# Two blocks of transformer layers on one core: half of some low weight parts on GpSimd, MLP sums kept in PSUM, all modulation sums on VectorE

## The chip, the cores and the metric

The kernel runs on one core of one Trainium2 chip. The metric is device time in microseconds (us) of one execution; lower is better. A difference of over 0.3% is about what a measurement of this kernel can tell.

## What is computed

Two blocks, one after the other, on a sequence of 256 tokens of width 1024, in float32.

The first block has two layers. Each is an adaptive norm (RMS norm, then a scale and a shift that come from a condition vector), an input projection of 4352 columns, two kinds of attention with 8 heads each, gates, an output projection, a second adaptive norm and an MLP of width 4096 with a squared ReLU. Cut to what matters here:

```python
mod = silu(c) @ w_ada + b_ada                  # 1024 x 6144: six chunks of 1024
sh1, sc1, gt1, sh2, sc2, gt2 = split(mod, 6)
h = rms_norm(x, g_mix) * (1 + sc1) + sh1
proj = h @ w_in                                # q, k, v of two attentions, two gates
mixed = sigmoid(gate_a) * (att_a @ w_o_swa) + sigmoid(gate_b) * (att_b @ w_o_moba)
x = x + gt1 * (mixed @ w_out)
h = rms_norm(x, g_mlp) * (1 + sc2) + sh2
x = x + gt2 * (square(relu(h @ w_up)) @ w_down)
```

The second block (a pooling layer and an attention layer, each with a mixture of experts) reads the result and a context of 256 more tokens. Its modulations are `silu(c) @ w_mod` for the tokens and `silu(c_ctx) @ w_mod` for the context. They depend on the inputs alone, so the kernel computes most of them while the first block runs.

## The kernel before, in words

**Units.** All weights come from HBM as 1 MB units, each 1024 rows by 256 columns (128 partitions x 2048 elements). Units 0 to 56 are layer 0 and 57 to 113 layer 1 of the first block: 9 of query, key and value projections, 8 of gates (with the attention beside them), 4 of the two attention outputs (each unit makes `y_a` and `y_b` of 256 columns), 4 of `w_out` ("out units") and 32 of the MLP. Unit 114 begins the second block.

**Two parts of a product.** A float32 product is made of three products of a rounded type: high x high, high x low and low x high. For each weight unit ScalarE writes the high part of the raw weights (L1449, `w_hi`, 128x2048), then VectorE subtracts it from the raw ones and writes the low part in two halves (L1946, `w_lo`, 128x1024 each). TensorE needs 48 matmuls of 256 columns for a unit (function `product`, L773). Three units can be split at a time (`w_hi`, `w_lo` have three places). Activations are split in the same way: ScalarE writes `h_hi`, `u_hi`, VectorE `h_lo`, `u_lo`.

**Modulations.** Each condition vector times a modulation matrix is done in pieces of 256 rows by 1024 columns (1 MB, an item `mod, layer, chunk, pair`; four pairs make a chunk; modulation layers 0 and 1 are `w_ada`, 2 and 3 are `w_mod`). For an item VectorE multiplies the two 128-row halves by the condition's columns and adds them into an accumulator (first one L1963, a `tensor_scalar`; the others L1969, a `scalar_tensor_tensor` from `raw` and `acc` into `acc`, 128x1024): 2 operations an item, 4 where the tokens and the context both need it (all of modulation layer 2, chunks 1 and 0 of layer 3). After four pairs TensorE sums the accumulators over the partitions (`sum_rows`), ScalarE copies the rows (L1436), TensorE turns them to columns (`sum_cols`) and VectorE adds the bias (L1925 to L1932). Eight items, chunks 1 and 0 of modulation layer 2, are taken another way: TensorE multiplies the raw items by the two conditions (`mod_product`, L726), in steps 75 to 79.

**Order.** `loading_order` (L251) writes one list of loads: weight units with modulation items between them, at a rate `pace` for each unit. SyncE's queue issues the loads into a ring of four 1 MB places (`raw`); load p waits until load p-4 has been used (`emptied`, L627). The list also says in which step (a unit of TensorE's order) ScalarE and VectorE deal with each item: a weight unit u in step u-2. VectorE works through a step's list in order, in `feed` (L1935), between its other work, and waits there for `w_hi`.

**Work beside the units.** While gates run, VectorE masks the scores (L2155), takes maxima (L2161) and normalises (L2098). In the mixing stage (attention outputs, then out units), VectorE makes `tanh(gate) + 1` times `y_a` and `y_b` (L2183), adds the two (L2188), feeds, and then writes the low part of the mix (L2200). The products of attention output unit j stand in PSUM banks 2(j mod 3) and the next one, those of out unit j in bank j. After an out unit VectorE adds it to `x` (L2085), ScalarE squares (L1474), GpSimd adds pairs of squares (L2543, `square_pair`) and TensorE sums them (`sum_pair`) for the next norm, one out unit behind. In the norm VectorE inverts the root (L1988) and writes scaled tokens (L2002) and low parts (L2011).

**MLP.** 16 "up" and 16 "down" units in four groups; the unit at place i writes bank i mod 4. After an up unit ScalarE takes ReLU (L1652), square and high part, and VectorE the low part two units later (L2213). After each down unit VectorE adds the product, scaled by the modulation, to `x` (L2085, two 128x256 operations): a tile of `x` gets four such additions, one a group.

GpSimd has little work in these layers: rotations of queries and keys (L2554, L2558) in steps 1 to 9 of a layer, and pairs of squares. In the expert part it makes four low parts of its own (L2640).

Of the kernel before, what the change touches and what calls it, by code (L numbers as in the profile page):

```python
# [242 lines left out]
PRODUCT_STEPS = (75, 75, 76, 76, 77, 78, 78, 79)  # L243


def two_fold(item):

    return item[0] == "mod" and item[1] == 2 and item[2] < 2


def loading_order():  # L251
# [4 lines left out]
    alone = [item for item in mods[:early] if not two_fold(item)]  # L256
    products = [item for item in mods[:early] if two_fold(item)]
    order, sent, due, step = [(-1, item) for item in alone[:8]], 8, 8.0, -1
    behind = iter(products)
# [33 lines left out]
class ModTable:  # L293
# [3 lines left out]
    def __init__(self, order):  # L297
        steps = range(-1, MOE1 + 1)
        self.feeds, self.rows, self.cols, self.products = ({step: [] for step in steps} for _ in range(4))
# [3 lines left out]
        for p, (step, item) in enumerate(order):  # L303
# [5 lines left out]
            if two_fold(item):  # L309
                self.products[step].append((p, item))  # L310
                if pair == 3:
                    assert not waiting and step % LAYER not in (*range(8, 17), 24, 55, 56)
                    batch = [(row, chunk) for _, row in conditions(layer, chunk)]
                    self.rows[step].append(len(self.batches))
                    self.cols[step + 1].append(len(self.batches))
                    self.batches.append(batch)
                continue
# [37 lines left out]
def build(nc, a, out):  # L355
    with ExitStack() as ctx:
# [339 lines left out]
        def tensor_program(e):  # L696
# [29 lines left out]
            def mod_product(p, item):  # L726

                _, layer, chunk, pair = item
                src = raw[:, p % RAW_SLOTS, :].rearrange("p (k c) -> p k c", c=D)
                if pair == 0:  # L730
                    claim(7)
                    e.wait_ge(*shaped.at("cond"))
                e.wait_ge(*in_raw[p % RAW_SLOTS].at(p, "all"))
                for k in range(2):
                    for half in range(2):
                        at_ = 32 * (2 * k + half)
                        d = mm(psum[at_:at_ + 2, 7, :], cond[:, 1:3, 2 * pair + k], src[:, k, half * 512:(half + 1) * 512],
                               pair == 0, pair == 3)
                d.then_inc(*summed.on("pair", p))
                if pair == 3:  # L740
# [2022 lines left out]
```

## Time and profile before

| what | us |
|---|---|
| median of three runs | 1636.26 (1632.52 to 1637.2) |
| the profiled execution | 1636.77 |
| its span, first to last instruction | 1635.0 |
| outside the span | 1.8 |
| layer 0 of the first block ends (last matmul of unit 56) | 450.2 |
| layer 1 ends (last matmul of unit 113) | 872.5 |

The rest of the span, from 872.5 us on, is the second block. The profile gives busy times for each engine (PE is TensorE's matmul, PEld its weight load, DVE VectorE, ACT ScalarE, POOL GpSimd). The matmuls are pipelined, so that PE counts as busy while it follows at its own pace. Unit ends are the ends of the last matmul of each unit. The granted clock of TensorE is 0.97 of full speed over the span.

### The profile page before, as it was taken

What the parts mean: (1) busy time and instruction counts of PE and PEld (TensorE: products, weight loads), DVE (VectorE), ACT (ScalarE), POOL (GpSimd) and SP (SyncE); (2) the same over time, 40 slices, a digit from 0 to 9 for tenths busy, and PEclk for the clock granted to TensorE, in tenths of its full rate; (3) what the DMA queues carried; (4) which work ended last, traced back from release to release, by engine and by line L of the source; (5) the groups of instructions that cost most, each with busy time, mean ns of one, the idle gap of its engine ahead of it and who ended that gap; (6) DMA issues with size and microseconds to landing.
All of it is one profiled execution on the core that took longest, in us unless ns stands there. A gap on an engine that the chain in (4) does not pass through costs nothing.

```text
span 1635.0 us, 24236 instructions
## 1 busy us (share of the span) xinstructions
PE 1532.5 (94%) x9886; PEld 1290.1 (79%) x9886; DVE 1233.5 (75%) x1857; ACT 836.5 (51%) x1164; POOL 212.3 (13%) x185
## 2 busy tenths in 40 slices
PE   3899989999999998999999999999989878899998
PEld 2889888999988986899998577777767746577775
DVE  5868798888887865799986587878757784387773
ACT  2537536444543752544545556666524465456661
POOL 5050000000005000000002300033210400300020
PEclk9999999999999999999999999999988989999999
DMA  9854497999955437687881489999964631489983
GB/s 325 275 157 131 155 322 266 332 312 321 324 186 161 147 125 273 219 283 269 299 305 63 162 337 371 374 354 364 367 218 144 218 128 60 157 341 368 356 326 116
DMA packets 184926, 409.12 MB, mean 250 GB/s; under 512 B 7576, under 2 KB 136016, under 8 KB 166256
## 3 DMA queue, kind: packets, MB, share of 16 engines
q1 hardware_dynamic: 170688, 334.53, 58.2%
q0 software_dynamic: 11200, 63.49, 10.8%
q10 hardware_dynamic: 2928, 9.57, 1.5%
q8 instruction: 78, 1.28, 0.3%
q14 instruction: 32, 0.26, 0.0%
HBM read 397.07 MB, written 10.49 MB: 249 GB/s over the span
## 4 chain that ended last, share of the span: by engine, by line
PE 76%; DVE 13%; ACT 5%; DMA 4%; issue 2%; POOL 0%; SPq 0%; ACTq 0%; DVEq 0%; POOLq 0%
PE psum L704 73%; DVE acc L1969 4%; DVE w_lo L1946 3%; DMA raw<-in_w_ada 1%; ACT w_hi L1449 1%; DMA raw<-in_w_down 1%; ACT att_room L1879 1%; DVE tmp L2002 1%; PE psum L1177 1%; PE psum L1210 1%; DVE h_lo L2011 1%; DVE tmp L2183 1%; DVE stats L2514 1%; PE psum L966 1%; DMA h_rows<-tmp 1%
## 5 line engine op out<-in xcount | busy, mean ns | idle before, releaser
L1946 DVE TENSOR_TENSOR w_lo<-raw,w_hi 128x1024 fp32r<-128x1024 f32 x250 | 304.5, 1260 | 72.9 <-ACT w_hi L1449 72.8
L704 PE MATMUL psum<-h_lo,w_hi 128*128 128x256 f32 (+1 forms) x1280 | 340.0, 289 | 0.0
L704 PE MATMUL psum<-h_hi,w_lo 128*128 128x256 f32 (+1 forms) x1280 | 339.8, 289 | 0.2 <-DVE w_lo L1946 0.2
L1449 ACT ACTIVATE w_hi<-raw 128x2048 fp32r<-128x2048 f32 x125 | 238.7, 1911 | 97.7 <-DMA raw<-in_w_up 43.5
L704 PE MATMUL psum<-h_hi,w_hi 128*128 128x256 f32 (+1 forms) x1280 | 263.6, 298 | 9.3 <-DVE tmp L2183 5.7
L1969 DVE SCALAR_TENSOR_TENSOR acc<-raw,cond,acc 128x1024 f32<-128x1024 f32 x196 | 258.4, 1326 | 10.7 <-DMA raw<-in_w_ada 6.2
L704 PEld LDWEIGHTS psum<-h_hi,w_lo 128*128 128x128 f32 x1280 | 249.3, 195 | 2.0 <-DVE w_lo L1946 0.7
L704 PEld LDWEIGHTS psum<-h_lo,w_hi 128*128 128x128 f32 x1280 | 249.5, 195 | 1.4
L1981 DVE TENSOR_TENSOR gu_lo<-raw,gu_hi 128x1024 fp32r<-128x1024 f32 x184 | 213.2, 1221 | 33.5 <-ACT gu_hi L1463 33.5
L704 PEld LDWEIGHTS psum<-h_hi,w_hi 128*128 128x128 f32 x1280 | 199.5, 196 | 32.8 <-issue 18.1
L1463 ACT ACTIVATE gu_hi<-raw 128x2048 fp32r<-128x2048 f32 x96 | 178.1, 1905 | 0.0
L704 PE MATMUL psum<-gu_hi,ht_lo 128*128 128x512 f32 x384 | 151.3, 394 | 0.5 <-DVE ht_lo L2420 0.5
L704 PE MATMUL psum<-gu_lo,ht_hi 128*128 128x512 f32 x384 | 151.6, 395 | 0.0
L704 PE MATMUL psum<-gu_hi,ht_hi 128*128 128x512 f32 x384 | 148.3, 406 | 2.3 <-issue 2.3
L704 PE MATMUL psum<-u_hi,w_lo 128*128 128x256 f32 x448 | 119.0, 283 | 0.0
L704 PE MATMUL psum<-u_lo,w_hi 128*128 128x256 f32 x448 | 119.0, 283 | 0.0
L704 PE MATMUL psum<-u_hi,w_hi 128*128 128x256 f32 x448 | 99.0, 286 | 0.0
L2543 POOL TENSOR_TENSOR tmp<-tmp 128x256 f32<-128x256 f32 (+1 forms) x28 | 29.1, 1041 | 494.1 <-ACT tmp L1474 494.1
L704 PE MATMUL psum<-dn_raw,ut_all 128*128 128x512 f32 x192 | 90.3, 592 | 1.2 <-ACT ut_all L1778 1.2
L704 PEld LDWEIGHTS psum<-gu_hi,ht_hi 128*128 128x128 f32 x384 | 73.2, 191 | 16.5 <-issue 2.6
L704 PEld LDWEIGHTS psum<-u_hi,w_lo 128*128 128x128 f32 x448 | 85.9, 192 | 0.0
L704 PEld LDWEIGHTS psum<-u_lo,w_hi 128*128 128x128 f32 x448 | 85.9, 192 | 0.0
(265 smaller groups left out, 2573.6 us busy)
## 6 DMA issues: line engine op xcount, KB each, us to landing
raw<-in_w_ada SPq DMA_DIRECT2D x48, 1024.0 KB, 6.9
raw<-in_w_mod SPq DMA_DIRECT2D x48, 1024.0 KB, 6.1
raw<-in_w_in SPq DMA_DIRECT2D x34, 1024.0 KB, 5.8
raw<-in_w_up SPq DMA_DIRECT2D x32, 1024.0 KB, 5.8
raw<-in_w_down SPq DMA_DIRECT2D x32, 1024.0 KB, 6.2
raw<-in_moe_wg SPq DMA_DIRECT2D x32, 1024.0 KB, 7.5
raw<-in_moe_wu SPq DMA_DIRECT2D x32, 1024.0 KB, 7.9
dn_raw<-in_moe_wd SPq DMA_DIRECT2D x32, 1024.0 KB, 7.2
```

The lines of the kernel that those rows point to most:

```text
L704: return e.matmul(o, lhs, rhs, start=start, stop=stop, skip_group_check=True)
L966: d = e.transpose(psum[:, b, j * P:(j + 1) * P], tbuf(h % 4)[:, first:first + P], ident)
L1177: d = e.transpose(psum[:, k // 4, k % 4 * P:(k % 4 + 1) * P], h_row[:, t % 3, k:D:DT], ident)
L1210: d = e.transpose(psum[:, 4, k * P:(k + 1) * P], tmp[:, s % 2, k:2 * P:2], ident)
L1449: e.activation(flat_unit(w_hi[:, split_slot(u)]), raw[:, slot, :], ACT.Copy).then_inc(*w_rounded.on(u))
L1463: e.activation(gate_up(0, s, kind == "u"), raw[:, p % RAW_SLOTS, :].rearrange("p (k c) -> p k c", c=UC), ACT.Copy).then_inc(*w_rounded.on( ...
L1879: e.activation(att_room[:, h % 4, qt * S2:(qt + 1) * S2], psum[:, 2 * (h % 2) + qt, :], ACT.Exp, bias=st[:, 2 + qt:3 + qt], scale=scale[:, ...
L1946: e.tensor_tensor(flat_unit(w_lo[:, split_slot(u), k]), raw[:, slot, part], plain(flat_unit(w_hi[:, split_slot(u), k])), ALU.subtract).the ...
L1969: e.scalar_tensor_tensor(out=a_buf, in0=src[:, k, :], scalar=s, in1=a_buf, op0=ALU.mult, op1=ALU.add).then_inc(*mod_v.on(p, n, k))
L1981: e.tensor_tensor(gate_up(1, s, kind == "u")[:, k], src[:, k], plain(gate_up(0, s, kind == "u")[:, k]), ALU.subtract).then_inc(*w_rest.on( ...
L2002: e.scalar_tensor_tensor(out=tmp[:, t % 4, c], in0=x[:, t, c], scalar=gain_col(row, chunk + 1, t), in1=psum[:, 5, c], op0=ALU.mult, op1=AL ...
L2543: e.tensor_tensor(o, o, tbuf(4 + (t + 1) % 4, n), ALU.add).then_inc(*pooled.on("sq", stage, t))
```

## The change

- `two_fold`, `PRODUCT_STEPS` and `mod_product` go: the eight items are treated like all others, by VectorE, with 4 operations each.
- `loading_order` gets other paces. Modulation items now also stand in the gates' steps of both layers and in layer 1's mixing stage. By the new list steps 82 to 108 of layer 1 hold 19 items with 4 VectorE operations each (before: 17), and steps 109 to 111 three (before: one). The number of loads is the same.
- The sums of chunks 4 and 3 for layer 0's second norm close in step 22 (before: 24). In layer 1's mixing stage two sums close (before three), one more in its MLP, and the last, of (3, 0), in step 113 (before 112).
- GpSimd writes the second half of the low part of the units 11 to 20 and 27 to 52 of each layer, 36 a layer, in order, each as soon as ScalarE has written the high part.
- MLP: down unit j of every group adds into bank j, and VectorE adds it to `x` once, after group 3. The up units take banks 4 and 5 in turn, the transposes of the context bank 6.
- Mixing stage: the out units take banks 2, 3, 0, 1. VectorE writes the low parts of mixes 2 and 3 after mix 3 and before the feed of step 20, which moves there and takes its weight unit first.

```diff
+    first = [0.5] * 3 + [0.8] * 6 + [0.4] * 8 + [0.5] * 4 + [0.25] * 2 + [0.5] * 2 + [0.85] * 32
+    second = [0.5] * 9 + [0.28] * 8 + [0.35] * 8 + [0.705] * 32
-    pace = [0.6] * 9 + [0.0] * 8 + [0.5] * 4 + [1.15] * 4 + [1.0] * 4 + [0.86] * 28
-            due = min(due + pace[u], 48) if u < LAYER else due + (0.5 if u < LAYER + 9 else 0.62 if u > LAYER + 23 else 0)
+        due = min(due + pace, 48) if u < LAYER else due + pace
...
+        OUT_BANKS = (2, 3, 0, 1)
...
+        def low_by_pool(u):
+            return u < POOL_UNIT and (11 <= u % LAYER <= 20 or 27 <= u % LAYER <= 52)
+        def unit_low(u, half):
+            return pooled.at("w_lo", u) if half and low_by_pool(u) else w_rest.at(u, half)
...
             if gone[0] == "w":
+                if low_by_pool(gone[1]):
+                    return [(w_rounded, gone[1:]), (w_rest, (gone[1], 0)), (pooled, ("w_lo", gone[1]))]
...
                     if what == "up":
+                        b = 4 + ups.index(i) % 2
                         product(gg, b, S, h_hi1, h_lo1, hi_ready, lo_ready)
                     else:
-                        product(gg, b, S, *((u_hiB, u_loB) if g % 2 == 0 else (u_hi1, u_lo1)),
+                        product(gg, j, S, *((u_hiB, u_loB) if g % 2 == 0 else (u_hi1, u_lo1)),
                                 lambda k: e.wait_ge(*rounded.at("u", l, g, k // 2)),
-                                lambda k: e.wait_ge(*rest.at("u", l, g, k // 2)))
-                        freed[b] = [(added, ("down", l, g, 2 * j + 1) if g < 3 else ("down", l, 2 * j + 1))]
+                                lambda k: e.wait_ge(*rest.at("u", l, g, k // 2)), g == 0, g == 3)
+                        if g == 3:
+                            freed[j] = [(added, ("down", l, 2 * j + 1))]
...
                     if item[0] == "w":
                         u = item[1]
                         e.wait_ge(*w_rounded.at(u))
-                        for half in range(2):
+                        for half in range(1 if low_by_pool(u) else 2):
...
+                def mix_low(q):
+                    ya = tbuf(2 * (q % 2)).rearrange("p (m n) -> p m n", n=S)
+                    c = slice(2 * q, 2 * q + 2)
+                    e.wait_ge(*rounded.at("mix", l, q))
+                    e.scalar_tensor_tensor(out=h_lo1[:, c, :], in0=ya, scalar=0.5, in1=plain(h_hi1[:, c, :]),
+                                           op0=ALU.mult, op1=ALU.subtract).then_inc(*rest.on("mix", l, q))
...
+                    if j == 4:
+                        mix_low(2)
+                        mix_low(3)
+                        late = table.feeds[g0 + 20]
+                        feed(g0 + 20, [f for f in late if f[1][0] == "w"] + [f for f in late if f[1][0] != "w"])
-                    if j < 8:
+                    if j < 8 and j != 3:
                         feed(g0 + 17 + j)
...
-                        if what == "down":
+                        if what == "down" and g == 3:
...
+            def low_half(u):
+                slot, k, part = ring_of["w", u], slice(DT // 2, DT), slice(UNIT // 2, UNIT)
+                e.wait_ge(*w_rounded.at(u))
+                e.tensor_tensor(flat_unit(w_lo[:, split_slot(u), k]), raw[:, slot, part],
+                                plain(flat_unit(w_hi[:, split_slot(u), k])), ALU.subtract).then_inc(*pooled.on("w_lo", u))
```

## Rows read from the trace of the kernel before

**Rows 1.** The page: busy times, then the chain that ended last, by engine.

```profile
PE 1532.5 (94%) x9886; PEld 1290.1 (79%) x9886; DVE 1233.5 (75%) x1857; ACT 836.5 (51%) x1164; POOL 212.3 (13%) x185
...
PE 76%; DVE 13%; ACT 5%; DMA 4%; issue 2%; POOL 0%; SPq 0%; ACTq 0%; DVEq 0%; POOLq 0%
```

**Rows 2.** Stages: window, length, busy PE, PEld, DVE, ACT, POOL (instructions), clock, DMA share, GB/s.

```profile
215.90:262.70 46.80, 39.27 (x284) 35.71 (x285) 40.51 (x56) 20.80 (x27) 4.94 (x6) 0.93 0.83 286
262.70:450.20 187.50, 187.50 (x1561) 184.30 (x1563) 159.51 (x171) 93.63 (x97) 2.68 (x3) 1.00 0.93 320
528.00:591.70 63.70, 63.15 (x531) 57.47 (x531) 54.64 (x154) 44.26 (x111) 0.00 (x0) 1.00 0.44 141
591.70:680.80 89.10, 79.53 (x592) 65.90 (x591) 51.87 (x82) 32.53 (x42) 3.53 (x4) 0.92 0.66 225
680.80:838.80 158.00, 158.00 (x1314) 154.11 (x1314) 155.56 (x167) 78.66 (x75) 0.00 (x0) 1.00 0.81 277
838.80:872.50 33.70, 32.08 (x268) 30.91 (x266) 22.84 (x27) 13.12 (x14) 4.97 (x5) 1.00 0.75 272
```

**Rows 3.** VectorE's groups by form (busy, mean ns, idle before), 680.8 to 838.8 us.

```profile
L1969 DVE SCALAR_TENSOR_TENSOR acc<-raw,cond,acc 128x1024 f32<-128x1024 f32 x59 | 74.6, 1282 | 1.2
L1946 DVE TENSOR_TENSOR w_lo<-raw,w_hi 128x1024 fp32r<-128x1024 f32 x52 | 61.2, 1219 | 1.3 <-ACT w_hi L1449 1.3
L2085 DVE SCALAR_TENSOR_TENSOR x<-psum,mod,x 128x256 f32<-128x256 f32 x22 | 9.6, 478 | 0.0
L1963 DVE TENSOR_SCALAR acc<-raw,cond 128x1024 f32<-128x1024 f32 x8 | 6.0, 748 | 0.0
```

**Rows 4.** Timeline (start, us): VectorE and POOL where both work, and apart.

```profile
92.36 3.45 DVE L1946 TENSOR_TENSOR w_lo<-raw,w_hi 128x1024 fp32r<-128x1024 f32 x2
498.87 7.95 DVE L1969 SCALAR_TENSOR_TENSOR acc<-raw,cond,acc 128x1024 f32<-128x1024 f32 x4
...
641.89 1.71 DVE L1969 SCALAR_TENSOR_TENSOR acc<-raw,cond,acc 128x1024 f32<-128x1024 f32 x1
...
682.98 5.12 DVE L1969 SCALAR_TENSOR_TENSOR acc<-raw,cond,acc 128x1024 f32<-128x1024 f32 x4
...
92.53 2.20 POOL L2558 TENSOR_TENSOR qk<-tmp 128x512 f32<-128x512 f32 x1 [0.90 <-DVE tmp L2036]
97.04 1.27 POOL L2558 TENSOR_TENSOR qk<-tmp 128x512 f32<-128x512 f32 x1
...
499.03 2.26 POOL L2558 TENSOR_TENSOR qk<-tmp 128x512 f32<-128x512 f32 x1 [0.90 <-DVE tmp L2036]
...
641.78 0.73 POOL L2543 TENSOR_TENSOR tmp<-tmp 128x256 f32<-128x256 f32 x1 [114.22 <-ACT tmp L1474]
```

**Rows 5.** POOL's groups by form: its low parts in the expert part.

```profile
L2640 POOL TENSOR_TENSOR gu_lo<-raw,gu_hi 128x1024 fp32r<-128x1024 f32 x8 | 18.6, 2355 | 0.0
```

**Rows 6.** Timeline of VectorE in layer 0's mixing stage and norm.

```profile
220.79 1.28 DVE L2183 SCALAR_TENSOR_TENSOR tmp<-gate_tanh,psum 128x512 f32<-128x512 f32 x2
222.10 0.69 DVE L2188 TENSOR_TENSOR tmp<-tmp 128x512 f32<-128x512 f32 x1
222.71 2.60 DVE L1969 SCALAR_TENSOR_TENSOR acc<-raw,cond,acc 128x1024 f32<-128x1024 f32 x2
225.29 2.36 DVE L1946 TENSOR_TENSOR w_lo<-raw,w_hi 128x1024 fp32r<-128x1024 f32 x2
227.56 0.68 DVE L2200 SCALAR_TENSOR_TENSOR h_lo<-tmp,h_hi 128x512 fp32r<-128x512 f32 x1
229.56 0.88 DVE L2085 SCALAR_TENSOR_TENSOR x<-psum,mod,x 128x256 f32<-128x256 f32 x2 [1.32 <-PE psum L704]
...
253.46 0.17 DVE L1928 SCALAR_TENSOR_TENSOR mod<-psum,par 128x8 f32<-128x8 f32 x1 [2.91 <-PE psum L704]
```

**Rows 7.** Layer 1's mixing stage: TensorE's products of modulations (group), VectorE (timeline).

```profile
L704 PE MATMUL psum<-raw,cond 128*2 128x512 f32 x64 | 9.9, 736 | 7.0 <-DMA raw<-in_w_mod 2.7 <-DVE mod L1925 2.4 <-DVE gain L1932 2.0
...
621.25 1.28 DVE L2183 SCALAR_TENSOR_TENSOR tmp<-gate_tanh,psum 128x512 f32<-128x512 f32 x2 [4.05 <-PE psum L704]
```

More of the change, by code:

```diff
@@ L239, in weight_units @@
     return units
-PRODUCT_STEPS = (75, 75, 76, 76, 77, 78, 78, 79)
-def two_fold(item):
-    return item[0] == "mod" and item[1] == 2 and item[2] < 2
 def loading_order():
@@ L255, in loading_order @@
     early = len(mods) - 16
-    alone = [item for item in mods[:early] if not two_fold(item)]
-    products = [item for item in mods[:early] if two_fold(item)]
+    alone = mods[:early]
     order, sent, due, step = [(-1, item) for item in alone[:8]], 8, 8.0, -1
-    behind = iter(products)
-    pace = [0.6] * 9 + [0.0] * 8 + [0.5] * 4 + [1.15] * 4 + [1.0] * 4 + [0.86] * 28
-    for u in range(POOL_UNIT + 1):
-        due = min(due + pace[u], 48) if u < LAYER else due + (0.5 if u < LAYER + 9 else 0.62 if u > LAYER + 23 else 0)
+    first = [0.5] * 3 + [0.8] * 6 + [0.4] * 8 + [0.5] * 4 + [0.25] * 2 + [0.5] * 2 + [0.85] * 32
+    second = [0.5] * 9 + [0.28] * 8 + [0.35] * 8 + [0.705] * 32
+    for u, pace in enumerate([*first, *second, 0.0]):
+        due = min(due + pace, 48) if u < LAYER else due + pace
         want = min(len(alone), int(due + 1e-6))
@@ L265, in loading_order @@
         sent = max(sent, want)
-        order += [(u - 3, item) for item in islice(behind, PRODUCT_STEPS.count(u - 3))]
         step = max(step, u - 2)
@@ L298, in __init__ @@
         steps = range(-1, MOE1 + 1)
-        self.feeds, self.rows, self.cols, self.products = ({step: [] for step in steps} for _ in range(4))
+        self.feeds, self.rows, self.cols = ({step: [] for step in steps} for _ in range(3))
         self.acc, self.before, self.last, self.previous = {}, {}, {}, {}
@@ L308, in __init__ @@
             _, layer, chunk, pair = item
[L309 to L317, printed above, removed]
             if pair:
@@ L724, in sum_rows @@
                 freed[7] = [(copied, ("mod_rows", n))]
[L726 to L734, printed above, removed]
-                    for half in range(2):
[L736 to L740, printed above, removed]
-                    n = table.batches.index([(row, chunk) for _, row in conditions(layer, chunk)])
-                    freed[7] = [(copied, ("mod_rows", n))]
             def sum_cols(n):
@@ L764, in close @@
                         sum_cols(n)
-                for p, item in table.products[g]:
-                    mod_product(p, item)
             def close_norm(g):
@@ L771, in close_norm, with product @@
                     sum_cols(n)
-            def product(g, b, n, hi, lo, hi_ready, lo_ready):
+            def product(g, b, n, hi, lo, hi_ready, lo_ready, first=True, last=True):
                 s, k_banks = split_slot(g), 2 * n // 512
                 o = psum[:, b:b + k_banks, :].rearrange("p b c -> p (b c)").rearrange("p (m n) -> p m n", n=n)
-                for i in range(k_banks):
-                    claim(b + i)
+                if first:
+                    for i in range(k_banks):
+                        claim(b + i)
                 e.wait_ge(*w_rounded.at(g))
@@ L784, in product @@
                             mm(o[:, m], w_hi[:, s, i, m * P:(m + 1) * P], hi[:, i, 0:n],
-                               i == 0 and (m == 0 or k_banks == 2), False)
+                               first and i == 0 and (m == 0 or k_banks == 2), False)
                     if i >= 1:
@@ L790, in product @@
                             mm(o[:, m], w_hi[:, s, k, m * P:(m + 1) * P], lo[:, k, 0:n], False, False)
-                            e.wait_ge(*w_rest.at(g, k // 4))
-                            d = mm(o[:, m], w_lo[:, s, k, m * P:(m + 1) * P], hi[:, k, 0:n], False, k == DT - 1)
+                            e.wait_ge(*unit_low(g, k // 4))
+                            d = mm(o[:, m], w_lo[:, s, k, m * P:(m + 1) * P], hi[:, k, 0:n], False,
+                                   last and k == DT - 1)
                 d.then_inc(*multiplied.on(g))
@@ L1432, in mod_rows_out @@
                     w = 32 * 2 * len(table.batches[n])
-                    e.wait_ge(*(summed.at("pair", paired[n]) if n in paired else summed.at("rows", n)))
+                    e.wait_ge(*summed.at("rows", n))
                     if n:
@@ L2600, in layer @@
                     rotate(l, j)
+                for u in range(g0 + 11, g0 + 21):
+                    low_half(u)
                 for j in range(9):
@@ L2609, in layer @@
                 nxt = ("a", 1) if l == 0 else ("p", 0)
+                for u in range(g0 + 27, g0 + 53):
+                    low_half(u)
                 for i in range(33):
```

46 lines of the change are left out of this document (15 added, 31 removed).

## The prediction

> **What bounds the kernel now.** I read the page first. TensorE is busy for 94% of the span, and the chain that ended last runs through it for 76%, through VectorE for 13% and through DMA for 4%; GpSimd (POOL in the rows) is busy for 212.3 of 1635 us [rows 1]. So GpSimd looks free, and what counts is where TensorE loses its own pace. The stages say that [rows 2]. In layer 1's MLP (680.8 to 838.8 us) TensorE works all 158.0 us; 1314 matmuls make 0.120 us each, 5.76 us for a unit's 48. Layer 0's MLP (262.7 to 450.2) is full in the same way. The stages around the mixing are not: 39.3 of 46.8 us in layer 0, 79.5 of 89.1 us in layer 1. A gain on TensorE's path has to come from there.
>
> The second thing to see is VectorE in layer 1's MLP: busy for 155.56 of 158.0 us, with 2.4 us of room. Its groups add up to that [rows 3]: 59 modulation operations of 1.28 us, 52 low halves of 1.22, 22 additions to x of 0.48, 8 first modulation operations of 0.75. In layer 0's MLP it is busy for 159.5 of 187.5 us, and the DMA engines are at 0.93. So any occupation of VectorE that grows by more than 2 us in layer 1's MLP comes out as time.
>
> The third is what happens when VectorE and GpSimd work at once [rows 4]. Two low halves take 2.36 us alone [rows 6] and 3.45 us at 92.36, where a GpSimd addition of 128x512 falls between them: +1.09. Four modulation operations take 5.12 us alone and 7.95 us at 498.87, where three GpSimd operations of 128x512 fall between them (the first at 499.03, the others the same way): +0.94 each. One with a GpSimd operation of 128x256 beside it takes 1.71 instead of 1.28: +0.43. GpSimd pays too: 2.20 and 2.26 us against 1.27 alone. The two lists of durations read like turns: each waits until the other's operation is done. So VectorE's price of a GpSimd operation is nearly that operation's length.
>
> **The change part by part.** Durations are those of the profiled execution (1636.77 us, span 1635.0, 1.8 us outside); the sum is made against it. It stands 0.5 us above the median of the three runs.
>
> (1) GpSimd's halves in layer 1's MLP. GpSimd alone needs 2.355 us for such a subtraction of 128x1024 [rows 5], well inside a unit's 5.76, so TensorE doesn't wait for GpSimd itself. What it takes from VectorE no row shows at this size. The bounds: nothing, if GpSimd always hits an idle VectorE; 2.355 us, if it holds it throughout. The rows give 0.43 us for 256 and 0.94 to 1.09 for 512 columns; drawn on to 1024 that is 2.0 to 2.2. I take 2.05, since VectorE is nearly never idle there. For 27 units of steps 82 to 108: +55.4 us on VectorE. It is relieved of 26 halves within the window (26 x 1.18 = 30.7, by the group's busy time over its count).
>
> The Trainium skill ("SBUF — State Buffer", section "SBUF: two separate sides") says that VectorE with two SBUF inputs and GpSimd take one port pair by an exclusive lock, held for the whole instruction. Turn-taking agrees with the rows; the whole 2.355 us would make this term 63.6 instead of 55.4, and the sum 8 us longer. No row here shows the hold at 1024 columns.
>
> (2) MLP sums in PSUM. The 22 additions in the window go: -9.7 us. The four additions at the end of the MLP stay. On TensorE nothing changes. With two banks for up units in place of four, ScalarE's ReLU of a unit must be done within the next unit's 5.76 us; ScalarE is busy for half of the time, so 0; and the same for one bank of transposes in layer 0.
>
> (3) More modulations. Steps 82 to 108 hold 19 items in place of 17, each of 4 operations: 8 more, about +9.6 us. Steps 109 to 111 hold two more, +10 us, of which the 10.9 us of idle time in 838.8 to 872.5 [rows 2] takes most; also TensorE does its last units there while VectorE has done.
>
> Layer 1's MLP: VectorE's 158 become 158 + 55.4 - 30.7 - 9.7 + 9.6 = 182.6. TensorE needs, with one more sum (2 us), 160. VectorE sets the pace, 6.7 us a unit. Net of about 3 us that the end gives back: **+22 us**. ScalarE's high parts and the ring of four loads follow VectorE there and add nothing.
>
> (4) Mixing, layer 0. Now a mix costs VectorE 1.28 + 0.69 + 2.60 + 2.36 + 0.68, 7.4 us with overlaps, against TensorE's 5.76 [rows 6]. So the last mix's low part ends at 228.2 us, and the first out unit at 229.5, where TensorE was done with the attention outputs at 215.9. After: the last y and its sum end at 217.9, the two low parts at 219.2, and the out unit (bank 2, long free) at 221.7, TensorE's own 5.76 us. That is -7.8. Some comes back: VectorE now has two low parts of units and a modulation item (2.36 + 2.60 + 2.36) before its first addition to x, so that it is done at 226.7; square and pair make it 228.5 to 229.2, where TensorE wants it at 227.5: +1.7. The sums for the second norm no longer stand in front of it: -1 (2.91 us of idle time before 253.46 [rows 6]). **-7.**
>
> (5) Mixing, layer 1. The products cost TensorE 9.9 us busy and 7.0 us of waits [rows 7]; both go, and the mixes follow the attention outputs closer (VectorE waited 4.05 us for one). Back come one sum of 1.2 us, and 4 operations each (4 to 5 us) of items in steps 72, 75, 78 and 80. In the gates' steps VectorE is at 54.6 of 63.7 us; half a unit's low part less, GpSimd's turn more and 1.3 us of modulation a unit bring it near 8.4 of TensorE's 8.25, and the item of step 72 makes the last normalisation, which nothing covers, some 3.5 us later. -16.9 + 1.2 + 3.5, rounded: **-12.**
>
> (6) Layer 0's MLP. Steps 25 to 50: VectorE 26 halves less (-30.7), about 22 additions less (-9.7), 26 turns more (+53): 159.5 becomes some 172 of 187.5. It fits, but the loop of the ring (load, high part, low part, next load) gets longer by 1.1 us at DMA 0.93. Bounds 0 and 12 (0.5 us a unit); I take **+5**, since the low part is about a unit ahead of TensorE today.
>
> (7) Queries and keys: three more operations of modulation beside GpSimd's rotations, **+1**. Last sum in step 113, in front of the norm: **+2**. The expert part is untouched; SyncE's queue issues the same loads.
>
> Sum: +22 - 7 - 12 + 5 + 1 + 2 = +11: 1636.8 + 11 = 1647.8, or 1647 against the median. Under 0.3%, 5 us, a measurement of this kernel cannot tell from no change.
>
> **The rivals.**
> - Faster (0.25): GpSimd's halves cost VectorE little, because the turn is short at this size or falls where VectorE has no SBUF pair to read. Then (1) is -30.7 and little more, VectorE needs about 127 + 10 of TensorE's 160 us, and the MLPs run at TensorE's pace: -7 - 16 - 1 + 2 and 0 to +2, 1613 to 1617. It decides where a turn costs under 1.2 us: 182.6 - 27 x 0.85 = 160. For it: the halves leave VectorE. Against: every overlap in the trace.
> - Same (0.13): turns of 1.4 to 1.8 us or larger gains in the mixing stages; 1632 to 1641.
> - Much slower (0.15, inside the slower ones): the turns also upset the ring in layer 0's MLP, where DMA is at 0.93; (6) then is 12 and more, and in layer 1 the hold is 2.355: 1660 to 1668.
> - That the change doesn't do what it says: the steps 82 to 108 might be bound by ScalarE's high parts. It is at 78.7 of 158 us; no chance of its own.
>
> **How the numbers follow.** Forecast 0.47, its own range 1641 to 1659 (turn 1.9 to 2.2, mixing 4 us either way); with the much slower case 0.62 for slower. Same 0.13. Faster 0.25. The range 1614 to 1662 leaves out the ends of both sides.
>
> **What would show it.** VectorE's groups in layer 1's MLP: w_lo halves and modulations with a mean well above 1.22 and 1.28 us, 27 new GpSimd operations of over 2.3 us, TensorE with idle time that the low parts end, and the stage near 180 in place of 158 us. The first out unit of layer 0 within 6 us of the attention outputs; no products in layer 1, and its mixing stage near 77 us. Wrong would be modulation operations that stay at 1.28 us beside GpSimd's, or a stage of 160 us.

## Result and the profile after

The changed kernel takes 1660.88 us (median of four runs, 1656.92 to 1662.76) against 1636.73 of the kernel before (four runs, 1632.52 to 1637.2): ratio 1.0157, 95% interval 1.014 to 1.0175, so slower by 24.1 us or 1.6%. The profiled execution took 1662.76 us with a span of 1661.0 (before 1635.0): +26.0. The sign was forecast, the size was not: +11. Line numbers shift: L1937 are the modulations (before L1969), L1916 VectorE's low halves (L1946), L2537 GpSimd's halves, L691 the matmuls (L704), L1419 `w_hi` (L1449), L2053 the additions to x (L2085), L2516 the pairs of squares (L2543).

The page of the changed kernel: busy times, and the chain by engine. They answer to [rows 1].

```profile
PE 1537.1 (93%) x9838; PEld 1299.3 (78%) x9838; DVE 1305.5 (79%) x1769; ACT 835.8 (50%) x1164; POOL 429.4 (26%) x257
...
PE 54%; DVE 31%; ACT 6%; DMA 5%; issue 3%; POOL 1%; SPq 0%; ACTq 0%; DVEq 0%; POOLq 0%
```

VectorE has 88 operations less and is busy 72 us longer; its share of the chain went from 13 to 31%. The stages of the changed kernel (columns as in [rows 2]; in order: layer 0's out units and norm, its MLP, layer 1's gates, its mixing stage, steps 83 to 108, 109 to 113):

```profile
212.01:256.97 44.96, 40.64 (x285) 36.68 (x284) 34.92 (x52) 21.02 (x27) 4.81 (x6) 0.92 0.69 233
256.97:448.62 191.65, 189.19 (x1561) 185.79 (x1563) 175.47 (x122) 93.72 (x97) 85.74 (x29) 0.99 0.92 313
525.00:590.70 65.70, 63.63 (x530) 57.42 (x530) 63.77 (x142) 42.07 (x103) 21.80 (x8) 1.00 0.51 166
590.70:670.46 79.76, 70.58 (x528) 63.65 (x528) 61.59 (x98) 33.27 (x49) 9.74 (x6) 0.94 0.53 174
670.46:856.30 185.84, 167.81 (x1317) 162.56 (x1319) 183.24 (x128) 78.74 (x77) 79.56 (x26) 0.94 0.74 251
856.30:893.50 37.20, 34.65 (x276) 33.28 (x279) 29.38 (x33) 13.13 (x14) 5.05 (x5) 0.95 0.81 283
```

The fifth line is the forecast's core: 158.0 us became 185.84, and VectorE is busy for 183.24 of them. Its groups there, then GpSimd's in 670.5 to 893.5 us (columns as in [rows 3]):

```profile
L1937 DVE SCALAR_TENSOR_TENSOR acc<-raw,cond,acc 128x1024 f32<-128x1024 f32 x66 | 116.6, 1785 | 1.3
L1916 DVE TENSOR_TENSOR w_lo<-raw,w_hi 128x1024 fp32r<-128x1024 f32 x28 | 47.0, 1687 | 0.4 <-ACT w_hi L1419 0.3
L1931 DVE TENSOR_SCALAR acc<-raw,cond 128x1024 f32<-128x1024 f32 x10 | 13.1, 1306 | 0.8 <-DMA raw<-in_w_mod 0.8
...
L2537 POOL TENSOR_TENSOR w_lo<-raw,w_hi 128x1024 fp32r<-128x1024 f32 x26 | 79.6, 3060 | 112.4 <-ACT w_hi L1419 112.4
```

The same operations took 1282, 1219 and 748 ns [rows 3]. TensorE now waits for VectorE there (670.5 to 893.5 us: who waited for whom, us in total, times, longest):

```profile
PE psum L691 <- DVE w_lo L1916: 7.6, 4, 3.2
PE psum L691 <- DVE u_lo L2190: 7.1, 1, 7.1
PE psum L691 <- DVE u_loB L2190: 3.3, 1, 3.3
```

These three are the 18.0 us for which TensorE is idle in steps 83 to 108. The timeline shows where the rest sits (start, length, VectorE's lines, then GpSimd's):

```profile
131.37 0.61 DVE L2129 TENSOR_REDUCE stats<-tmp 128x1 f32<-128x128 f32 x2
132.01 1.76 DVE L2134 TENSOR_SCALAR stats<-stats,sink 128x2 f32<-128x2 f32 x1
...
735.09 7.17 DVE L1937 SCALAR_TENSOR_TENSOR acc<-raw,cond,acc 128x1024 f32<-128x1024 f32 x4
742.17 4.55 DVE L1916 TENSOR_TENSOR w_lo<-raw,w_hi 128x1024 fp32r<-128x1024 f32 x2
...
131.34 2.40 POOL L2537 TENSOR_TENSOR w_lo<-raw,w_hi 128x1024 fp32r<-128x1024 f32 x1 [5.15 <-ACT w_hi L1419]
...
738.14 3.02 POOL L2537 TENSOR_TENSOR w_lo<-raw,w_hi 128x1024 fp32r<-128x1024 f32 x1 [5.98 <-ACT w_hi L1419]
742.25 3.40 POOL L2537 TENSOR_TENSOR w_lo<-raw,w_hi 128x1024 fp32r<-128x1024 f32 x1 [1.08 <-ACT w_hi L1419]
```

Four modulation operations with one GpSimd half among them take 7.17 us instead of 5.12 [rows 4], two low halves 4.55 instead of 2.36 [rows 6]: +2.05 and +2.19 a turn. GpSimd waits too: 3.02 and 3.40 us for an operation of 2.40. The first two lines are taken up in the last section.

The span by stages, from the ends of the units, with the forecast of each difference:

| stage | before | after | measured | forecast |
|---|---|---|---|---|
| layer 0, units 0 to 8 | 122.3 | 119.3 | -3.0 | +1 |
| layer 0, gates | 64.9 | 64.9 | 0 | 0 |
| layer 0, attention outputs to norm | 75.5 | 72.8 | -2.7 | -7 (4) |
| layer 0, MLP | 187.5 | 191.6 | +4.1 | +5 (6) |
| layer 1, norm to second norm | 230.6 | 221.8 | -8.7 | -12 (5) |
| layer 1, MLP (units 83 to 113) | 191.7 | 223.0 | +31.3 | +22 (1 to 3), +2 last sum |
| second block | 762.5 | 767.5 | +5.0 | 0 |

### The profile page after: what moved, and what is told of

The parts are those of the page before. It is cut to its first block, busy times and chain, and to the rows that moved or that the text cites. A ratio compares the mean times of both kernels' runs of the same rounds, so it can differ in the third digit from the quotient of the medians.

```text
span 1661.0 us, 24077 instructions
## 1 busy us (share of the span) xinstructions
PE 1537.1 (93%) x9838; PEld 1299.3 (78%) x9838; DVE 1305.5 (79%) x1769; ACT 835.8 (50%) x1164; POOL 429.4 (26%) x257
## 4 chain that ended last, share of the span: by engine, by line
PE 54%; DVE 31%; ACT 6%; DMA 5%; issue 3%; POOL 1%; SPq 0%; ACTq 0%; DVEq 0%; POOLq 0%
PE psum L691 52%; DVE acc L1937 12%; DVE w_lo L1916 7%; ACT w_hi L1419 2%; DMA raw<-in_w_ada 1%; DVE tmp L2123 1%; DVE stats L2129 1%; DVE tmp L1970 1%; ACT att_room L1849 1%; DVE h_lo L1979 1%; DMA raw<-in_w_up 1%; DVE tmp L2066 1%; DVE acc L1931 1%; PE psum L1147 1%; PE psum L1180 1%
## 5 line engine op out<-in xcount | busy, mean ns | idle before, releaser
L1937 DVE SCALAR_TENSOR_TENSOR acc<-raw,cond,acc 128x1024 f32<-128x1024 f32 x224 | 355.6, 1596 | 12.7 <-DMA raw<-in_w_ada 7.7
L691 PE MATMUL psum<-h_hi,w_lo 128*128 128x256 f32 (+1 forms) x1280 | 342.2, 290 | 6.7 <-DVE w_lo L1916 6.7
L691 PE MATMUL psum<-h_lo,w_hi 128*128 128x256 f32 (+1 forms) x1280 | 341.9, 290 | 0.5 <-DVE h_lo L2148 0.5
L1419 ACT ACTIVATE w_hi<-raw 128x2048 fp32r<-128x2048 f32 x125 | 238.8, 1912 | 157.8 <-DMA raw<-in_w_up 86.8
L2537 POOL TENSOR_TENSOR w_lo<-raw,w_hi 128x1024 fp32r<-128x1024 f32 x72 | 216.9, 3013 | 319.4 <-ACT w_hi L1419 319.4
L1916 DVE TENSOR_TENSOR w_lo<-raw,w_hi 128x1024 fp32r<-128x1024 f32 x178 | 250.0, 1430 | 59.1 <-ACT w_hi L1419 58.8
L691 PE MATMUL psum<-h_hi,w_hi 128*128 128x256 f32 (+1 forms) x1280 | 264.4, 299 | 3.5 <-ACT h_hi L1459 2.5
L691 PEld LDWEIGHTS psum<-h_hi,w_lo 128*128 128x128 f32 x1280 | 251.2, 196 | 9.0 <-DVE w_lo L1916 7.6
L691 PEld LDWEIGHTS psum<-h_lo,w_hi 128*128 128x128 f32 x1280 | 251.1, 196 | 2.0 <-DVE h_lo L2148 0.7
L691 PEld LDWEIGHTS psum<-h_hi,w_hi 128*128 128x128 f32 x1280 | 200.9, 197 | 24.4 <-issue 14.4
L691 PE MATMUL psum<-gu_hi,ht_lo 128*128 128x512 f32 x384 | 150.8, 393 | 0.5 <-DVE ht_lo L2393 0.5
L691 PE MATMUL psum<-gu_lo,ht_hi 128*128 128x512 f32 x384 | 151.1, 394 | 0.0
L691 PE MATMUL psum<-gu_hi,ht_hi 128*128 128x512 f32 x384 | 147.9, 405 | 2.3 <-issue 2.3
L691 PE MATMUL psum<-u_lo,w_hi 128*128 128x256 f32 x448 | 120.9, 287 | 7.1 <-DVE u_lo L2190 7.1
L691 PE MATMUL psum<-u_hi,w_lo 128*128 128x256 f32 x448 | 120.7, 286 | 1.0 <-DVE w_lo L1916 1.0
L691 PE MATMUL psum<-u_hi,w_hi 128*128 128x256 f32 x448 | 100.1, 289 | 0.0
L691 PEld LDWEIGHTS psum<-u_lo,w_hi 128*128 128x128 f32 x448 | 87.5, 195 | 7.3 <-DVE u_lo L2190 7.3
L691 PE MATMUL psum<-dn_raw,ut_all 128*128 128x512 f32 x192 | 90.3, 592 | 1.9 <-ACT ut_all L1748 1.9
L2516 POOL TENSOR_TENSOR tmp<-tmp 128x256 f32<-128x256 f32 (+1 forms) x28 | 28.5, 1017 | 239.9 <-ACT tmp L1444 239.8
L691 PEld LDWEIGHTS psum<-u_hi,w_lo 128*128 128x128 f32 x448 | 87.4, 195 | 1.2 <-DVE w_lo L1916 1.2
```

The costliest lines, as they stand in the source:

```text
L691: return e.matmul(o, lhs, rhs, start=start, stop=stop, skip_group_check=True)
L1419: e.activation(flat_unit(w_hi[:, split_slot(u)]), raw[:, slot, :], ACT.Copy).then_inc(*w_rounded.on(u))
L1916: e.tensor_tensor(flat_unit(w_lo[:, split_slot(u), k]), raw[:, slot, part], plain(flat_unit(w_hi[:, split_slot(u), k])), ALU.subtract).the ...
L1937: e.scalar_tensor_tensor(out=a_buf, in0=src[:, k, :], scalar=s, in1=a_buf, op0=ALU.mult, op1=ALU.add).then_inc(*mod_v.on(p, n, k))
L2516: e.tensor_tensor(o, o, tbuf(4 + (t + 1) % 4, n), ALU.add).then_inc(*pooled.on("sq", stage, t))
L2537: e.tensor_tensor(flat_unit(w_lo[:, split_slot(u), k]), raw[:, slot, part], plain(flat_unit(w_hi[:, split_slot(u), k])), ALU.subtract).the ...
```

## Experiments

Ratios are to the kernel before on the same chip. Its medians beside the runs were 1632.7 to 1636.7 us.

**The parts one by one.** First the changed kernel without GpSimd's halves, so that VectorE makes all low parts:

```diff
-            return u < POOL_UNIT and (11 <= u % LAYER <= 20 or 27 <= u % LAYER <= 52)
+            return False
...
-                for u in range(g0 + 11, g0 + 21):
-                    low_half(u)
...
-                for u in range(g0 + 27, g0 + 53):
-                    low_half(u)
```

> The changed kernel with all low parts back on VectorE. Theory (turns): each GpSimd half took about 2.1 us of VectorE's time and relieved it of 1.2, so layer 1's MLP loses 27 x 2.1 = 57 us of waiting and gets 31 us of work back, near 160 us, TensorE's own pace; layer 0's MLP loses some 4 us, the gates' steps some 5. In all 1617 to 1632 us, below both kernels. Rival (the 40 us of modulation work that moved to VectorE are the cost): 1650 us or more.

Measured: 1631.52 us, ratio 0.998 (0.9968 to 0.9992): 29 us below the changed kernel, at the upper end of the theory. Layer 1's MLP fell from 223.0 to 199.3 us, not to the kernel before's 191.7. Of the 7.7 us left, 4.1 are in steps 83 to 108, where VectorE is full without any turn, and 3.5 in the last five units. Its groups and the window of these steps (this kernel; both views):

```profile
L1937 DVE SCALAR_TENSOR_TENSOR acc<-raw,cond,acc 128x1024 f32<-128x1024 f32 x65 | 82.2, 1282 | 1.4
L1916 DVE TENSOR_TENSOR w_lo<-raw,w_hi 128x1024 fp32r<-128x1024 f32 x54 | 63.4, 1218 | 2.7 <-ACT w_hi L1419 2.7
```

```profile
662.60:824.70 162.10, 158.72 (x1316) 154.09 (x1318) 158.02 (x153) 78.34 (x75) 0.00 (x0) 1.00 0.84 291
```

The means are back at 1282 and 1218 ns: what the changed kernel's operations had gained in length was all GpSimd's doing. From the means of the changed kernel: 66 x (1.785 - 1.282) + 28 x (1.687 - 1.219) + 10 x (1.306 - 0.748) = 51.9 us for the three groups, and 2.1 for the low parts of activations (14 operations, 11.7 us instead of 9.6), is 54.0 over 26 halves, 2.08 us each.

Then the halves alone in the kernel before:

```diff
+            return u < POOL_UNIT and (11 <= u % LAYER <= 20 or 27 <= u % LAYER <= 52)
...
-                        for half in range(2):
+                        for half in range(1 if low_by_pool(u) else 2):
```

> The kernel before with GpSimd's 72 halves alone. Turns: layer 1's MLP gets 27 x (2.1 - 1.2) = 25 us longer, with 2 us in layer 0's MLP and 1 to 3 us in the gates: 1655 to 1672 us. Rival (the halves relieve VectorE, the loss comes from elsewhere): 1630 to 1638 us.

Measured: 1669.26 us, ratio 1.0217 (1.0203 to 1.0232). Layer 1's MLP takes 28.2 us more here too (191.7 to 219.9), so the turns need nothing else of the change; the whole is inside the theory's range. The sums in PSUM alone, with the up units' banks that they need:

```diff
-                        if what == "down":
+                        if what == "down" and g == 3:
```

> The kernel before with the MLP's sums in PSUM alone. VectorE gets 10 us of room in each MLP, where TensorE sets the pace: 1633 to 1638 us. Rival (two banks for the up units make TensorE wait for ScalarE's ReLU): over 1640 us, with waits of the up units' first matmuls for ScalarE.

Measured: 1633.88 us, ratio 0.9997 (0.9987 to 1.0007): no difference; VectorE is busy for 18 us less over the span (1215.2 of 1631.1), which the kernel before doesn't need. The mixing stage's banks and order alone:

```diff
-                    b = j
+                    b = OUT_BANKS[j]
...
+                    if j == 4:
+                        mix_low(2)
+                        mix_low(3)
+                        late = table.feeds[g0 + 20]
+                        feed(g0 + 20, [f for f in late if f[1][0] == "w"] + [f for f in late if f[1][0] != "w"])
```

> The kernel before with the mixing stage's other banks and other order alone. Theory: layer 0 gains about 7 us there, layer 1 some 4 (the products stay in its way): 1622 to 1631 us. Rival (the add to x and its square become late, and take all back): 1634 to 1638 us.

Measured: 1639.29 us, ratio 1.0029 (1.0016 to 1.0042): slower by 0.3%, so the rival, and 1.3 us beyond its range. The first out unit of layer 0 did take 7.9 us less (13.66 to 5.76 us, as forecast), but the third and fourth took 5.5 and 3.7 us more. In layer 1 nothing was won: its first out unit took 15.5 us instead of 11.3, its third 10.2 instead of 11.6. The window from the attention outputs to the fourth out unit, in the kernel before:

```profile
215.90:247.70 31.80, 26.18 (x204) 25.96 (x208) 29.62 (x32) 12.47 (x13) 4.22 (x5) 0.89 0.96 328
```

and in this one, with TensorE's timeline behind the second and the third out unit, VectorE's up to the additions to x, and ScalarE's high part of the fourth:

```profile
214.10:247.25 33.15, 27.45 (x205) 26.91 (x207) 30.27 (x32) 12.78 (x13) 4.20 (x5) 0.90 0.92 326
```

```profile
229.44 0.61 PE L705 MATMUL psum<-cst,tmp 128*128 128x1 f32 x4 [3.79 <-POOL tmp L2553]
239.30 0.61 PE L705 MATMUL psum<-cst,tmp 128*128 128x1 f32 x4 [1.92 <-POOL tmp L2553]
...
220.55 4.00 DVE L1970 SCALAR_TENSOR_TENSOR acc<-raw,cond,acc 128x1024 f32<-128x1024 f32 x3
224.47 2.35 DVE L1947 TENSOR_TENSOR w_lo<-raw,w_hi 128x1024 fp32r<-128x1024 f32 x2
226.74 0.87 DVE L2086 SCALAR_TENSOR_TENSOR x<-psum,mod,x 128x256 f32<-128x256 f32 x2
...
234.78 2.36 DVE L1947 TENSOR_TENSOR w_lo<-raw,w_hi 128x1024 fp32r<-128x1024 f32 x2 [1.61 <-ACT w_hi L1450]
237.06 0.87 DVE L2086 SCALAR_TENSOR_TENSOR x<-psum,mod,x 128x256 f32<-128x256 f32 x2
...
232.84 1.91 ACT L1450 ACTIVATE w_hi<-raw 128x2048 fp32r<-128x2048 f32 x1 [4.78 <-DMA raw<-in_w_out]
```

TensorE waits for GpSimd's pairs of squares, 3.79 and 1.92 us, and each pair waits for VectorE's additions to x. This is the mechanism that the rival named. The first additions stand behind an item and two low halves in a VectorE that was already busy for 29.6 of the stage's 31.8 us. The second stand behind low halves that waited 1.61 us for the high part, which had waited 4.78 us for its load (the DMA engines stood at 0.96 in this stage before). The rest, 1.7 us in each of the two units, is a stretch of 3.4 us at a granted clock of 1.2 GHz (from 230.2 and 240.4 us) behind each wait. Is the gain there under the new paces? The changed kernel without GpSimd's halves, with the banks of before:

```diff
-        OUT_BANKS = (2, 3, 0, 1)
+        OUT_BANKS = (0, 1, 2, 3)
```

and with the kernel before's order of low parts and feeds (the edit above, undone).

> The changed kernel without GpSimd's halves and with the banks and the order of the mixing stage of before; left of the change are the paces (with the products gone) and the sums in PSUM. Theory: the new order pays only with the new paces, which leave fewer modulation operations between the last mix and the first addition to x, so this is 5 to 12 us slower than the kernel without halves (1637 to 1643), with the first out unit of layer 0 back at 12 to 14 us. Rival: the paces alone give the gain, and this stays within 3 us of it (1629 to 1634).

Measured: 1641.26 us, ratio 1.0049 (1.0034 to 1.0064), 9.7 us above the median of the kernel without halves: the theory. With fewer items in the stage (VectorE busy for 22.1 of 27.3 us, DMA at 0.78) the same order pays 8.3 and 8.5 us at the first out units of the two layers; 1 us is lost again in a later out unit and 3.4 to 3.8 in the norm of each. Of the 8.3, 5.7 are the wait; most of the rest is a stretch of 6.8 us at 1.2 GHz that begins during it (218.6 us; in the kernel before at 218.9 us).

**Where turns cost time.** Halves everywhere but in layer 1's MLP:

```diff
-            return u < POOL_UNIT and (11 <= u % LAYER <= 20 or 27 <= u % LAYER <= 52)
+            return u < POOL_UNIT and (11 <= u % LAYER <= 20 or 27 <= u <= 52)
```

> The changed kernel with GpSimd's halves in all its units but those of layer 1's MLP (46 of 72 halves). Theory: turns cost time only where VectorE is full; then layer 1's MLP takes 197 to 201 us in place of 223, the rest stands as in the changed kernel, and the whole takes 1634 to 1641 us. Rival: the halves cost about the same everywhere, 29.4 us over 72 halves, 0.41 us each; then 46 of them leave 1650 us.

Measured: 1641.43 us, ratio 1.0043 (1.0029 to 1.0056), 0.4 us above the theory's range and far from the rival's 1650. Layer 1's MLP takes 199.9 us, as without any halves; so its 26 halves cost 23 us, 0.9 each, the other 46 some 8 us (from the medians, 1641.43 against 1631.52, less the first units), 0.2 each: 4.2 in layer 0's MLP, 1.9 in layer 1's gates, 1.7 in layer 0's out units and norm (1.7 more lie in the first units, where no half is). Both "only where VectorE is full" and "0.41 each" were too simple.

**The length of a turn.** Each half in four operations of 256 columns:

```diff
-                e.tensor_tensor(flat_unit(w_lo[:, split_slot(u), k]), raw[:, slot, part],
+                for k in range(DT // 2, DT):
+                    e.tensor_tensor(flat_unit(w_lo[:, split_slot(u), k:k + 1]), raw[:, slot, k * UC:(k + 1) * UC],
```

> The changed kernel with each of GpSimd's halves made in four operations of 128x256. Theory: a turn is as long as GpSimd's operation, whatever its size, so that four short ones cost VectorE together about what the long one does (4 x 0.43 to 0.55): 1656 to 1666 us, with VectorE's modulation operations and low halves in layer 1's MLP at means of 1.6 to 1.8 us. Rival one: a short operation slips into the gaps between VectorE's, and costs it little: below 1648 us. Rival two: each handing over costs a fixed time: above 1668 us.

Measured: 1658.44 us, one run, inside the theory's range. Layer 1's MLP, VectorE's groups and GpSimd's:

```profile
L1937 DVE SCALAR_TENSOR_TENSOR acc<-raw,cond,acc 128x1024 f32<-128x1024 f32 x67 | 107.9, 1627 | 1.3
L1916 DVE TENSOR_TENSOR w_lo<-raw,w_hi 128x1024 fp32r<-128x1024 f32 x28 | 47.8, 1716 | 1.0 <-ACT w_hi L1419 1.0
...
L2538 POOL TENSOR_TENSOR w_lo<-raw,w_hi 128x256 fp32r<-128x256 f32 x104 | 156.6, 1539 | 31.8 <-ACT w_hi L1419 31.8
```

The two engines take turns, operation by operation: VectorE's are longer by 0.35 and 0.5 us on average, and each short GpSimd operation lasts 1.54 us (another addition of that size took 0.73 [rows 4]), since it waits for one of VectorE's. Over the two groups VectorE loses 67 x (1.627 - 1.282) + 28 x (1.716 - 1.219) = 37.0 us, against 33.2 + 13.1 = 46.3 in the changed kernel. With the first modulation operations (2.9 us) and the low parts of activations (6.4 us, three times as much as there) it is 46.3 against 54.0: four short turns cost 86% of a long one. GpSimd now needs some 6.2 us for a half. Layer 0's MLP takes 196.6 us (4.9 more than in the changed kernel), layer 1's 214.8 (8.2 less).

**Placing the items.** With no halves, the question left was what makes layer 1's MLP 199.3 us, and whether the change's good parts can be kept. Only the list of layer 1's items is written by hand (their positions are units, two above the step):

```diff
-    second = [0.5] * 9 + [0.28] * 8 + [0.35] * 8 + [0.705] * 32
+    second = [[1, 3, 4, 5, 6, 7, 9, 10, 13, 15, 20, 22, 29, 30, 32, 33, 35, 36, 38, 39, 41, 42, 44, 45, 47, 48, 50, 51, 53, 54, 55, 56].count(u) for u in range(LAYER)]
```

> The changed kernel without GpSimd's halves, with layer 1's modulation items placed by hand: eight in steps 56 to 65, two in the gates' steps 68 and 70 (none in step 72), two in the mixing stage, 17 in steps 84 to 108, three in steps 109 to 111. Theory: without the halves it is the number of items that fills VectorE in layer 1's MLP (158 of 162 us there, 199.3 us for the 31 units where TensorE needs 191), and the item of step 72 that makes the last normalisation late (6.6 us at the first attention output). Then the MLP takes 191 to 194 us, that output 5 to 7 us less, and the whole 1614 to 1623 us, below both kernels. Rival: the items only move the time to the steps of the projections, where VectorE has 48.4 of 62.6 us busy and gets 15 more; then these take 5 to 8 us more and the whole stays at 1626 to 1633.

Measured: 1630.76 us, ratio 0.9973 (0.9961 to 0.9985). The MLP came to 192.8 us and the first attention output to 11.2 (from 16.8), as the theory said; but the units of the projections and gates took 11.5 us more (81.3 and 70.4 us against 76.0 and 64.2), as the rival said. The third out unit took 13.0 us instead of 7.2, the norm's unit 12.1 instead of 17.8. A better choice of steps:

```diff
+    second = [[1, 2, 3, 4, 5, 6, 7, 10, 14, 20, 23, ...
```

> As the first placing by hand, with the items moved to the steps that cost nothing in the traces so far: seven in steps 56 to 62, none in 64 and 65's neighbour, 65 and 69 in the gates (as in the kernel without halves, but without 72), 75 and 78 in the mixing stage (77 made the first addition to x 5 us late), 18 in layer 1's MLP and three in steps 109 to 111. Theory: each step of the projections and the gates can take an item at no cost only where VectorE's own work of that step leaves 5 us within two steps; then units 64 to 73 lose nothing (11 us less than in the first placing), unit 74 stays near 11 us, the MLP takes 192 to 195 us, and the whole 1616 to 1622 us. Rival: the total of VectorE's work in layer 1 sets the time, wherever the items stand: 1626 to 1632.

Measured: 1625.93 us, ratio 0.9953 (0.9936 to 0.997). The gates are back at 65.1 us, but the projections keep 81.0; the loss only moved from units 64 and 65 to 60 and 63. The theory holds for the gates alone, and the whole is at the rival's lower end (1626), above the theory's 1616 to 1622 us. The item of step 77 was blamed wrongly: without it the third out unit and the norm take 13.1 and 12.1 us, 25.2 together, against 25.1 with it and 24.9 in the kernel without halves; a wait for squares had moved from the one to the other (2.9 us in the out unit with the item, 3.0 in the norm of the kernel without halves). Then one item of layer 0 from step 24 to step 7:

```diff
-    first = [0.5] * 3 + [0.8] * 6 + [0.4] * 8 + [0.5] * 4 + [0.25] * 2 + [0.5] * 2 + [0.85] * 32
+    first = [[1, 3, 4, 6, 7, 8, 9, 10, 13, 15, 17, 19, 22, 24, 27, ...
```

> As the second placing, with one more item moved in layer 0, from step 24, where it stands in front of the last addition to x and of the norm, to step 7. Theory: the last addition comes 2.5 to 3 us earlier, and so does the norm: 2 to 3 us less than the second placing. Rival: the norm waits for the low halves or the squares instead: no difference.

Measured: 1624.14 us, ratio 0.9945 (0.9927 to 0.9963). The fourth out unit of layer 0 fell from 9.7 to 6.5 us, as forecast, but 2.1 of it went into a sum of chunks that moved from step 22 to 19, where TensorE has no wait to hide it; with medians 1.8 us apart the runs don't tell the two kernels apart. Last, the last sum:

```diff
-    second = [[1, 2, 3, 4, 5, 6, 7, 10, 14, 20, 23, 29, 31, ...
+    second = [[1, 2, 3, 4, 5, 6, 7, 10, 14, 20, 23, 29, 30, ...
```

> As the third placing, with the last items one step earlier (19 in steps 84 to 108, two in 109 and 110), so that the last sum stands in step 112, as in the kernel before, and not in 113. Theory: with the sum in 113 its transposes come in step 114 behind ScalarE's copies of the tokens, where TensorE waits 2.5 us for them and takes 1.5 us; with the sum in 112 that wait is gone, and the stretch from unit 114 to the routing falls from 59 to 61 us to 55 to 58; the whole 1620 to 1624 us. Rival: the longer stretch is half-rate matmuls alone, which come and go; then it stays at 59 to 61 us, with the same 2.5 us wait or another in its place, and the nineteenth item makes the MLP longer: 1624 to 1628.

Measured: 1623.0 us, ratio 0.9918 (0.9903 to 0.9933), 13.6 us below the kernel before beside it: the lowest of all, though its interval and that of the placing before overlap. TensorE after unit 114 in the changed kernel, timeline:

```profile
917.43 1.51 PE L691 MATMUL psum<-cst,v_tok 128*128 128x4 f32 x8 [2.52 <-ACT by_token L1663]
918.80 6.82 PE L691 MATMUL psum<-window_tab,by_token 128*128 128x136 f32 x32
```

and in this one:

```profile
879.14 3.87 PE L691 MATMUL psum<-window_tab,by_token 128*128 128x136 f32 x32
```

The wait of 2.5 us and the transposes of the last sum are gone from there; unit 114 to the routing takes 56.1 us (changed kernel 60.5, the placing before 60.8, the kernel before 56.1). Every kernel with the last sum in step 113 shows the 2.5 us wait. Of the 4.7 us, some 4 are the sum's and the rest is the clock: the placing before spent 2.3 us more on these 32 matmuls at 1.2 GHz, this one 1.5 us more further on. The nineteenth item costs 1.8 us in the MLP (198.5 against 196.7), as the rival said.

## Why the prediction was right in sign and wrong in size

- **(1), the turn: right.** Taken at 2.05 us for 1024 columns, measured 2.08 a half in layer 1's MLP (2.05 and 2.19 in the two turns shown). The Trainium skill ("SBUF — State Buffer", "SBUF: two separate sides") has the lock held for the whole instruction; GpSimd's takes 2.36 us [rows 5], and VectorE lost 0.2 to 0.3 less, so the full length would have been too much. The term was 55.4 us (27 units) and came to 54.0 (26 halves).
- **(1) to (3), the stage: too small by 9.3 us against +22 (7.3 with the +2 of the last sum).** The main step that failed is "net of about 3 us that the end gives back": the last five units took 37.2 us instead of 33.7, so 3.5 us more and not 3 less. TensorE's own work there is 34.65 instead of 32.08 us, and it waits 2.5 instead of 1.6 us for the squares. With the same items, but no halves and no half-rate stretch (a stretch in which TensorE's granted clock is 1.2 GHz; the kernel with the banks of before has none there) the five units take 35.7 us: so some 2 us are the items and their sum, and 1.5 the matmuls at 1.2 GHz (3.4 us from 887.1). The kernel without halves has the same 37.2, but the halves alone in the kernel before, with its one item, give 37.5 with 6.8 us at 1.2 GHz, so the turns are not cleared. The second step was a size: 182.6 us for steps 83 to 108, measured 185.84, by VectorE's work and not by its idle time (2.6 us, before 2.44). The relief was put at 26 halves (30.7 us), but 54 halves fall in the stage, not 52, and VectorE is relieved of 24 (28.3). The modulations cost 10.5 us, not 9.6. About 1.3 us stay open. TensorE's clock went down inside the stage as well (three stretches of 6.8 us at 1.2 GHz and one of 3.4, none before), where VectorE set the pace; what that adds is not told apart.
- **(2) alone: right.** The sums in PSUM are worth nothing in the kernel before.
- **(4), mixing in layer 0: -2.7 instead of -7.** The first out unit gave its part (-7.1 of -7.8), though 2.2 of it is a half-rate stretch that stood there before (6.8 us from 218.9) and now stands in the fourth (from 235.2). The step that failed was "some comes back: +1.7, -1": the third and fourth out units took 2.2 and 6.0 us more, the norm 2.9 less. The late squares cost less than forecast, 0.94 us of wait. But the sums for the second norm didn't vanish from TensorE's path: they moved from the norm into the out units, 1.1 us in the third, and in the fourth 1.2 us of transposes behind a wait of 1.8 us for ScalarE's copy. That copy stands behind a chain that begins with a load for which ScalarE waits 3.07 us. [rows 2] gave the DMA share with the norm, 0.83; without the norm it was 0.96, and the prediction had no term for such a load.
- **(5), layer 1 up to its second norm: -8.7 instead of -12.** The products and their waits went as forecast (units 76 to 81: -16.2, forecast -16.9 + 1.2). The first attention output came 5.7 us later, where 3.5 was forecast: TensorE's wait for the last normalisation is 3.80 us, near the forecast, and 1.7 of the rest is a half-rate stretch behind it (3.4 us from 597.0). The gates took 2.0 us more, forecast "near 8.4 of 8.25 a unit", the norm another 1.2, and the projections 1.4 less.
- **(6), layer 0's MLP: +4.1, forecast +5**, all of it at unit 35, and in part by the mechanism named: ScalarE had waited 5.23 us for a load before the high part, and TensorE waits 2.5 us for the copy that ScalarE makes next. The rest is a half-rate stretch (3.4 us from 313.7).
- **(7) and the second block.** The last sum was put at +2 in front of a norm; it landed behind ScalarE's copies in step 114, where nothing was forecast: 2.5 us of wait and 1.5 of transposes, shown by the last run. Half-rate matmuls there (6.82 us instead of 3.87 for the same 32) add 3.0; against them stand 1.1 us less of wait for the squares and 1.5 us of a half-rate stretch that the kernel before had at 942.5 us. In the first units a half-rate stretch of the kernel before (6.8 us from 68.7, TensorE busy throughout) is missing, and a longer one stands where TensorE works for 13.3 of 27.3 us: -3.0, which no term forecast. Such stretches fall elsewhere from kernel to kernel; one execution of each was traced, and a few us of any single profile are theirs.

Of the 15 us missed, 7.3 are in layer 1's MLP, 5.0 in the second block, 4.3 in (4), 3.3 in (5), and -4.9 in the first units and (6). The sign and the turn were foreseen; that the time still fell inside the range, at its edge (1660.9 of 1662), is luck in part, since -3.0 us came from the clock in the first units. The "much slower" case had the right time for the wrong reason, a hold of 2.355 us and 12 us and more in layer 0's MLP (4.1 measured).

## What to carry to other kernels

Work given to GpSimd is not free for a VectorE that reads two operands from SBUF: price each GpSimd operation at nearly its own length on VectorE, and compare it with what it relieves VectorE of (here 2.08 against 1.18 us). Before crediting a shorter wait on TensorE's path, read the other engines' work in just that stretch, without the norm behind it: with VectorE busy for 29.6 of 31.8 us and DMA at 0.96 the gain came back as waits for VectorE's additions, one of them held up by a load. And where paces change, follow the last item to the step in which its sum and its transposes are done.

## What the runs showed of the hardware

The turn does not depend on the size of VectorE's operation: a `TENSOR_SCALAR` of 128x2, 0.23 us elsewhere, took 1.76 us and ended with GpSimd's operation (132.01 + 1.76 against 131.34 + 2.40). Nor does it need two operands from SBUF, as the prediction had put it: six `TENSOR_SCALAR` of 128x2 with one operand and a constant (L2137, 0.17 us elsewhere) took 1.01 to 1.71 us, and each ended within 0.04 us after GpSimd's. Two `TENSOR_REDUCE` ran beside the same GpSimd operation at their usual length (0.61 us together, from 131.37). Which property of the form decides was not tried. And a GpSimd operation cut in four gets its turns one by one between VectorE's, so that GpSimd's part grows from 3.06 to 4 x 1.54 us while VectorE loses a seventh less (46.3 instead of 54.0 us).
